# Modulation units of 2 row blocks x 512 columns, two at a time on four column groups; bias rows written later

## Chip, core and metric

The program runs on one core of one Trainium2 chip, in one launch. The metric is the device time of an execution in microseconds (us). The core has a matrix engine (PE, with its weight loads shown apart as PEld), a vector engine (DVE), a scalar engine (ACT), GpSimd (POOL), a queue engine that only issues transfers (SP), and 16 DMA engines that serve all queues.

## Reference

Two layers of a diffusion backbone over 256 latent and 256 context tokens, 1024 wide, in float32. Each layer is feed-forward, token mixing, feed-forward, and each of these is modulated by vectors that come from a conditioning vector. What the change touches is the product that makes these vectors, and the bias table of one of the attentions:

```
c_act = jax.nn.silu(c);  cc_act = jax.nn.silu(c_ctx)
mod  = (c_act  @ lp['w_mod'] + lp['b_mod'])      # w_mod: 1024 x 9216 per layer
modc = (cc_act @ lp['w_mod'] + lp['b_mod'])
ada = lambda t, g, shift, scale: rms_norm(t, g) * (1 + scale) + shift
x = x + 0.5 * m(2) * ffn(ada(x, lp['norm_ffn1'], m(0), m(1)), 'ffn1')
...
bias = rpb[:, dr[:, None, None, :, None], dc[None, :, :, None, :]]
```

## The kernel before

Activations lie transposed: features on the 128 partitions, tokens in columns, 512 columns for both streams. All weights stream from DRAM through four slots `raw[0..3]` of 512 KB, in one fixed order of **units** that `plan_units` lists; unit u uses slot u % 4. SP issues one load for each unit, in order, and waits before it until the slot's last user is through: for a modulation unit until PE has done it (`unit_done`), for a product unit until DVE has made its low part (`lo_made`).

**A product unit** is 1024 rows x 128 columns of a weight. ACT rounds it to `w_hi` (`split_hi`, L631), DVE makes `w_lo` (L641), both two units ahead of PE, and PE does 24 matmuls of 512 columns in the fast float32 format (L690, L691, L696).

**A modulation unit** is 1024 rows x 128 columns of `w_mod`, used by PE as it lands and in full float32: `modulation` (L798) holds a 32 column weight `cact` (the two conditioning vectors, padded with zeros) and streams the 128 columns, once for each of 8 row blocks k. Row block k writes to the 32 output rows of column group k % 4 of PE, so that four partial sums stand in `bank[7]`; the order list has 8 matmuls for such a unit. After four units the bank is full (512 columns). ACT copies it to `mod_row` (L1216), POOL stores the rows to DRAM (L1903), and PE may write the bank again only when it is copied (`mod_copied`, waited for by the first unit of each four). The rows are loaded back later, turned and added up by PE (`turn_modulation`, L810), and DVE makes the vectors of them.

There are 144 modulation units. The first 16 stand alone at the start (the opening), where nothing else can begin before them: two for each eighth of the inputs, which PE turns between them (L974). The other 128 are spread among the gate and up products of the feed-forwards, by the table `MOD_AT`: one modulation unit ahead of each product ("step 2") in seven parts, 104 units in all, and two ahead of each product ("step 3") in one part, 24 units:

```
MOD_AT = {(0, 1, 0): (0, 16, 1), (0, 1, 1): (0, 32, 2), (0, 1, 2): (0, 56, 1),
          (0, 2, 0): (1, 0, 1), (0, 2, 1): (1, 16, 1), (0, 2, 2): (1, 28, 1),
          (1, 1, 0): (1, 44, 1), (1, 1, 1): (1, 60, 1)}
```

The key is (layer, feed-forward, part). A part runs in turns of four products, j = 0 to 3 (gate, up, gate, up), four turns or three. In a turn ACT does in this order: for j = 0 and 2 `split_hi` two products ahead and then SiLU of the gate product (L1203); for j = 1 and 3 `split_hi` and then the rounding of the inner product (L1206). The copy of a full bank stands ahead of the work of j = 3 with step 2, and of j = 1 and j = 3 with step 3, behind the SiLU. The first two products of a feed-forward are done together, block by block as the norm delivers (`first_pair`, L763, L764, L769); with step 2 one modulation unit stands ahead of them and one among them.

POOL also writes the bias rows, a spread copy of `na_rpb`, to DRAM by 8 transfers (L2012); they are read only in the mixing of layer 0.

Of the kernel before, what the change touches and what calls it, by code (L numbers as in the profile page):

```python
# [25 lines left out]
P = 128  # L26
# [142 lines left out]

HALVED = [(0, (1, 2)), (0, "out"), (0, (2, 2)), (1, (1, 2))]  # L170
# [15 lines left out]
def plan_units():  # L186
# [7 lines left out]
    for l in range(LAYERS):  # L194
        if l == 0:
            stage("mod", MOD_FIRST, "mod", DC)
        for ffn in (1, 2):
# [8 lines left out]
            for part, (_, n) in enumerate(PARTS):  # L206
                first["up", l, ffn, part] = len(units)
                for _ in range(2 * n):
                    if (l, ffn, part) in MOD_AT:
                        units.extend(Unit("mod", DC, 1) for _ in range(MOD_AT[l, ffn, part][2]))  # L210
                    units.append(Unit("product", DC, 1))
                stage(("down", l, ffn, part), sweep_steps(l, (ffn, part)), "product", n)
# [10 lines left out]
def build(nc, values, x, c, ctx_tokens, c_ctx, w_mod, b_mod, norm_ffn1, ffn1_w_gate, ffn1_w_up, ffn1_w_down,  # L223
# [7 lines left out]
    with ExitStack() as ctx:  # L231
# [303 lines left out]
        def _(sp):  # L535
# [6 lines left out]
            def load(u, i, per, *sources):  # L542
# [11 lines left out]
                for rows, src in sources:  # L554
                    sp.dma_start(raw[unit.slot][:, rows[0]:rows[1], :], src).then_inc(loaded[unit.slot], 16)
# [16 lines left out]
            for l in range(LAYERS):  # L572
                if l == 0:
                    stage(first["mod"], MOD_FIRST, lambda j: [((0, DC), columns(w_mod, 0, j * P))])
                for ffn in (1, 2):
# [16 lines left out]
                    for part, (c0, n) in enumerate(PARTS):  # L592
# [6 lines left out]
                        def turn_loads(i, per):  # L599
                            for j in range(4):  # L600
                                for q in range(ahead):
                                    load(u0 + step * j + q, i, per, ((0, DC), columns(
                                        w_mod, extra[0], i * (4 * ahead * P) + (extra[1] + ahead * j + q) * P)))
                                load(u0 + step * j + step - 1, i, per,
                                     ((0, DC), columns((wg, wu)[j % 2], l, i * (2 * P) + (c0 + j // 2) * P)))
# [48 lines left out]
        def at(u0, j, i, step=1):  # L654

            j = step * j + step - 1
# [20 lines left out]
        def _(pe):  # L677
# [110 lines left out]
            def modulation(u, i, per, j, m):  # L788
# [25 lines left out]
            def up(l, ffn, part, n):  # L814
# [9 lines left out]
                def body(i):  # L824
                    start = 0
                    if part == 0 and isinstance(i, int) and i == 0:
                        m0 = mod_first.get((l, ffn, part))
                        if step == 2:
                            modulation(u0, 0, (0, 0), 0, m0)
                        for j in range(2):  # L830

                            pe.wait_ge(silu_done if j == 0 else inner_made, c0)
                        first_pair(at(u0, 0, 0, step), at(u0, 1, 0, step), n, (l, ffn),
                                   (lambda: modulation(u0 + 2, 0, (0, 0), 1, m0)) if step == 2 else None)
# [1230 lines left out]
```

## Time and profile before

| | |
|---|---|
| median of 3 runs | 2385.78 us (2379.91 to 2389.27) |
| profiled execution | 2382.76 us, span 2380.8 us |
| PE busy | 2257.0 us, 95% |
| PE weight loads / DVE / ACT / POOL busy | 78% / 50% / 38% / 10% |
| PE clock granted, mean | 0.98 |
| DMA | 340.83 MB, mean 143 GB/s |

Busy time is that of the profiled execution, and its span leaves out some 2 us around it. PE is nearly always busy, so that time can be won only in PE's own work or in its few stretches of waiting.

### The profile page before, as it was taken

The numbers are of one execution on the slowest core, as the hardware profiler recorded it, in microseconds if no ns is written. First come the engines' busy times: TensorE is split into PE (matmuls) and PEld (weight loads), VectorE is DVE, ScalarE is ACT, GpSimd is POOL, SyncE is SP. The second block draws the span as 40 slices with busy tenths as digits, with TensorE's granted clock in tenths as the row PEclk, the third lists the DMA queues.
The fourth block names the chain that finished last, engine by engine and source line by source line (L and its number), as shares of the span: only waits on it lengthen the run. The fifth ranks groups of instructions, "written<-read, shape, count | busy, mean of one in ns | idle before, by whom it ended". The sixth has DMA issues, their size and how long they took to land. (4 is left out here: it accounts for less than half of the span.)

```text
span 2380.8 us, 36412 instructions
## 1 busy us (share of the span) xinstructions
PE 2257.0 (95%) x14113; PEld 1851.9 (78%) x14113; DVE 1179.6 (50%) x1848; ACT 902.6 (38%) x1415; POOL 238.2 (10%) x347
## 2 busy tenths in 40 slices
PE   4999899999999989999999999999999899988998
PEld 3777677888766667877777797777889777788998
DVE  1432232496377546743333364333337848775554
ACT  2321222353455442532222253222235446634444
POOL 2000000150000001200000020000005101110000
PEclk8999999999999999999999999999999999989999
DMA  9554746553333335555454655545335445564663
GB/s 275 149 165 125 190 126 175 165 133 102 93 100 97 93 107 150 153 152 164 116 152 137 171 165 157 158 119 155 111 97 153 119 109 144 146 182 142 179 181 119
DMA packets 618095, 340.83 MB, mean 143 GB/s; under 512 B 15307, under 2 KB 609719, under 8 KB 617815
## 3 DMA queue, kind: packets, MB, share of 16 engines
q1 hardware_dynamic: 603648, 305.18, 45.9%
q0 software_dynamic: 12848, 29.37, 4.5%
q10 hardware_dynamic: 1446, 4.18, 0.5%
q8 instruction: 104, 1.70, 0.3%
q14 instruction: 49, 0.39, 0.0%
HBM read 326.50 MB, written 12.94 MB: 143 GB/s over the span
## 5 line engine op out<-in xcount | busy, mean ns | idle before, releaser
L641 DVE TENSOR_TENSOR w_lo<-raw,w_hi 128x1024 fp32r<-128x1024 f32 (+1 forms) x444 | 544.5, 1227 | 925.2 <-ACT w_hi L631 539.6
L631 ACT ACTIVATE w_hi<-raw 128x1024 fp32r<-128x1024 f32 (+1 forms) x444 | 462.4, 1041 | 951.8 <-PE bank L691 366.1
L690 PE MATMUL bank<-h_hi,w_hi 128*128 128x512 f32 (+1 forms) x1856 | 661.4, 368 | 12.0 <-DVE h_lo L1510 10.7
L691 PE MATMUL bank<-h_lo,w_hi 128*128 128x512 f32 (+1 forms) x1856 | 643.2, 359 | 0.0
L690 PEld LDWEIGHTS bank<-h_hi,w_hi 128*128 128x128 f32 x1856 | 354.2, 191 | 86.4 <-issue 34.6
L696 PE MATMUL bank<-h_hi,w_lo 128*128 128x512 f32 (+1 forms) x1856 | 395.5, 356 | 5.1 <-DVE w_lo L641 5.1
L691 PEld LDWEIGHTS bank<-h_lo,w_hi 128*128 128x128 f32 x1856 | 355.6, 192 | 48.2 <-issue 0.5
L696 PEld LDWEIGHTS bank<-h_hi,w_lo 128*128 128x128 f32 x1856 | 314.2, 190 | 54.5 <-DVE w_lo L641 5.9
L690 PE MATMUL bank<-inner_hi,w_hi 128*128 128x256 f32 (+1 forms) x896 | 270.7, 327 | 11.3 <-DVE inner_lo L1575 10.9
L691 PE MATMUL bank<-inner_lo,w_hi 128*128 128x256 f32 (+1 forms) x896 | 268.8, 324 | 0.0
L690 PEld LDWEIGHTS bank<-inner_hi,w_hi 128*128 128x128 f32 x896 | 169.0, 189 | 30.9 <-DVE inner_lo L1575 15.1
L705 PE MATMUL bank<-h_hi,w_hi 128*128 128x512 f32 (+1 forms) x512 | 169.9, 351 | 12.1 <-ACT wa L1369 7.7
L691 PEld LDWEIGHTS bank<-inner_lo,w_hi 128*128 128x128 f32 x896 | 169.2, 189 | 15.4
L706 PE MATMUL bank<-h_lo,w_hi 128*128 128x512 f32 (+1 forms) x512 | 165.0, 341 | 0.0
L696 PE MATMUL bank<-inner_hi,w_lo 128*128 128x256 f32 (+1 forms) x896 | 163.8, 324 | 0.0
L696 PEld LDWEIGHTS bank<-inner_hi,w_lo 128*128 128x128 f32 x896 | 134.3, 189 | 15.3
L1903 POOL DMA_DIRECT2D mod_rows<-mod_row x72 | 40.6, 565 | 965.9 <-ACT mod_row L1216 964.2
L705 PEld LDWEIGHTS bank<-h_hi,w_hi 128*128 128x128 f32 x512 | 98.3, 192 | 46.7 <-ACT gstage L1369 19.1
L798 PE MATMUL bank<-raw,cact 128*32 128x128 f32 x2304 | 96.7, 293 | 31.0 <-DMA raw<-in_w_mod_dram 19.5
L1206 ACT ACTIVATE inner_hi<-wb 128x512 fp32r<-128x512 f32 (+3 forms) x88 | 50.9, 579 | 177.9 <-DVE wb L1571 177.9
L798 PEld LDWEIGHTS bank<-raw,cact 128*32 128x32 f32 x2304 | 59.2, 115 | 75.2 <-issue 60.1
L1591 DVE SCALAR_TENSOR_TENSOR X<-bank,gatev,X 128x256 f32<-128x256 f32 x192 | 87.9, 479 | 46.3 <-PE bank L696 46.0
(226 smaller groups left out, 2407.3 us busy)
## 6 DMA issues: line engine op xcount, KB each, us to landing
raw<-in_w_mod_dram SPq DMA_DIRECT2D x144, 512.0 KB, 4.0
raw<-in_w_in_dram SPq DMA_DIRECT2D x108, 512.0 KB, 4.0
raw<-in_ffn_w_gate_dram SPq DMA_DIRECT2D x88, 512.0 KB, 4.9
raw<-in_ffn_w_up_dram SPq DMA_DIRECT2D x88, 512.0 KB, 4.9
raw<-in_ffn_w_down_dram SPq DMA_DIRECT2D x88, 512.0 KB, 4.1
raw<-in_ffn_w_down_dram SPq DMA_DIRECT2D x32, 384.0 KB, 3.5
raw<-in_w_out_dram SPq DMA_DIRECT2D x24, 512.0 KB, 4.1
raw<-in_w_branch_dram SPq DMA_DIRECT2D x16, 512.0 KB, 5.2
```

Of the source, the lines that this page charges most:

```text
L631: act.activation(w_hi[n % 2][:, 0:unit.rows, :], raw[unit.slot][:, 0:unit.rows, :], ACT.Copy).then_inc(hi_made, 1)
L641: dve.tensor_tensor(w_lo[n % 2][:, 0:unit.rows, :], raw[unit.slot][:, 0:unit.rows, :], w_hi[n % 2][:, 0:unit.rows, :].bitcast(F32), ALU.su ...
L690: pe.matmul(psum, w_hi[s][:, row0 + k, :], hi, start=(k == 0), stop=False)
L691: mm = pe.matmul(psum, w_hi[s][:, row0 + k, :], lo, start=False, stop=False)
L696: mm = pe.matmul(psum, w_lo[s][:, row0 + k, :], rhs(k)[0], start=False, stop=(k == rows - 1))
L705: pe.matmul(psum, w_hi[s][:, k, :], h_hi[:, k, 0:n], start=(k == 0), stop=False)
L706: mm = pe.matmul(psum, w_hi[s][:, k, :], h_lo[:, k, 0:n], start=False, stop=False)
L798: mm = pe.matmul(bank[7][rows, j * P:(j + 1) * P], cact[:, k, :], raw[unit.slot][:, k, :], start=(k < 4), stop=(k >= 4))
L1206: act.activation(inner_hi[:, bass.ds(i * 2 + j // 2, 1), 0:n], wb[:, (j // 2) % 2:(j // 2) % 2 + 1, 0:n], ACT.Copy).then_inc(inner_hi_made, 1)
L1591: ins = dve.scalar_tensor_tensor(out=X[:, d % DC, stream_cols(st)], in0=bank[4 + d % 2][:, stream_cols(st)], scalar=gatev[:, gate_i, d % D ...
L1903: pool.dma_start(mod_rows[l, s, :, bass.ds(chunk0 * P, 4 * P)], mod_row[s::32, :]).then_inc(mod_stored, 16)
```

## The change

A modulation unit now has 2 row blocks x 512 columns, where it had 8 row blocks x 128. Four units still make a full bank: unit 4a + j of them holds row blocks 2j and 2j + 1 of the same 512 columns. It has 2 matmuls of 512 columns, to two of the four column groups: units 0 and 2 of a four to groups 0 and 1, units 1 and 3 to groups 2 and 3. In DRAM the pieces of a load are 2 KB long, where they were 512 bytes. With step 2 the order of a turn becomes two modulation units and then two products (`TURN_ORDER`); with step 3 it stays as it was. The two modulation units of the first two products now both stand ahead of them. The 8 transfers of the bias rows move in POOL's program from behind the load of the first vectors to behind the load of portion (0, "gate"), in the feed-forward.

```diff
+TURN_ORDER = {1: ["p0", "p1", "p2", "p3"],
+              2: ["m0", "m1", "p0", "p1", "m2", "m3", "p2", "p3"],
+              3: ["m0", "m1", "p0", "m2", "m3", "p1", "m4", "m5", "p2", "m6", "m7", "p3"]}
...
+def in_turn(step, kind, j):
+
+    return TURN_ORDER[step].index(kind + str(j))
...
+                    dst = raw[unit.slot][:, rows[0]:rows[1], :]
+                    if unit.kind == "mod":
+                        dst = raw[unit.slot][:, :, :].rearrange("p r c -> p (r c)").rearrange("p (k n) -> p k n", k=2)
+                    sp.dma_start(dst, src).then_inc(loaded[unit.slot], 16)
+
+            def mod_rows_of(l, col, a):
+
+                return w_mod[l].rearrange("(k p) n -> p k n", p=P)[:, 2 * a:2 * a + 2, bass.ds(col, 4 * P)]
...
-                for k in range(DC):
+                two = raw[unit.slot][:, :, :].rearrange("p r c -> p (r c)").rearrange("p (k n) -> p k n", k=2)
+                for k in (2 * j, 2 * j + 1):
                     rows = slice(32 * (k % 4), 32 * (k % 4) + 32)
-                    mm = pe.matmul(bank[7][rows, j * P:(j + 1) * P], cact[:, k, :], raw[unit.slot][:, k, :],
-                                   start=(k < 4), stop=(k >= 4))
+                    mm = pe.matmul(bank[7][rows, :], cact[:, k, :], two[:, k % 2, :], start=(k < 4), stop=(k >= 4))
...
-                        m0 = mod_first.get((l, ffn, part))
-                        if step == 2:
-                            modulation(u0, 0, (0, 0), 0, m0)
+                        for q in range(2 * (step - 1)):
+                            modulation(u0 + in_turn(step, "m", q), 0, (0, 0), q % 4, mod_first[l, ffn, part] + q // 4)
...
-            for l in range(LAYERS):
-                for h in range(4):
-
-                    row = na_rpb[l, h, NA_ROWS - ROWS, 0:1]
-                    src = bass.AP(row.tensor, row.offset, [[2 * NA_COLS - 1, 2 * ROWS - 1], [0, GRID_W], [1, P]])
-                    rows_written.done(pool.dma_start(bias_rows[l, h], src), "all")
             for key in sorted(MOD_AT):
                 l, chunk0, ahead = MOD_AT[key]
                 if key == (0, 1, 1):
                     load_modulation(0, "gate")
+                    write_bias_rows()
```

On PE, in the first turn with step 2 (part (0, 1, 0)), the order before, from the end of the first two products (L763 to L769) on, is a modulation unit, a product (L690, L691, L696), a modulation unit, a product:

```order
L798 MATMUL bank<-raw,cact 32x128 x8
L690 MATMUL bank<-h_hi,w_hi 128x512
L691 MATMUL bank<-h_lo,w_hi 128x512
...
L696 MATMUL bank<-h_hi,w_lo 128x512 x8
L798 MATMUL bank<-raw,cact 32x128 x8
L690 MATMUL bank<-h_hi,w_hi 128x512
L691 MATMUL bank<-h_lo,w_hi 128x512
...
L696 MATMUL bank<-h_hi,w_lo 128x512 x8
```

and at the same place of the changed kernel, whose lines L817, L708, L709 and L714 are L798, L690, L691 and L696 of before:

```order
L817 MATMUL bank<-raw,cact 32x512 x4
L708 MATMUL bank<-h_hi,w_hi 128x512
L709 MATMUL bank<-h_lo,w_hi 128x512
...
L714 MATMUL bank<-h_hi,w_lo 128x512 x8
L708 MATMUL bank<-h_hi,w_hi 128x512
L709 MATMUL bank<-h_lo,w_hi 128x512
...
L714 MATMUL bank<-h_hi,w_lo 128x512 x8
```

Two units of 8 short matmuls have become 4 long ones in a row, and the two products stand next to each other.

On SP, the loads of that part's first turn before:

```order
L555 DMA raw<-in_w_mod_dram 128x8x128
L555 DMA raw<-in_ffn_w_gate_dram 128x8x128
L555 DMA raw<-in_w_mod_dram 128x8x128
L555 DMA raw<-in_ffn_w_up_dram 128x8x128
```

and in the changed kernel, where the first row also holds the 16 units of the opening:

```order
L567 DMA raw<-in_w_mod_dram 128x2x512 x18
L567 DMA raw<-in_ffn_w_gate_dram 128x8x128
L567 DMA raw<-in_ffn_w_up_dram 128x8x128
L567 DMA raw<-in_w_mod_dram 128x2x512 x2
```

The gate load now stands behind two modulation loads, where one was ahead of it.

On POOL, the transfers around the load of the first vectors before:

```order
L1914 DMA scores<-mod_rows 16x8x128
L2012 DMA bias_rows<-in_na_rpb_dram 448x1x128 x8
L2028 UNCONDITIONAL_BRANCH
```

and in the changed kernel, around the second such load, one loop of stores later:

```order
L1933 DMA scores<-mod_rows 8x8x128
L1954 DMA bias_rows<-in_na_rpb_dram 448x1x128 x8
L2051 UNCONDITIONAL_BRANCH
```

The 8 transfers now follow the modulation stores of part (0, 1, 0) and stand ahead of those of part (0, 1, 1).

## Rows read from the trace of the kernel before

**Rows 1.** The page: span, busy time and share of each engine
```profile
span 2380.8 us, 36412 instructions
PE 2257.0 (95%) x14113; PEld 1851.9 (78%) x14113; DVE 1179.6 (50%) x1848; ACT 902.6 (38%) x1415; POOL 238.2 (10%) x347
```

**Rows 2.** PE by time, step 2: start, us, line, tiles, count
```profile
131.71 0.51 PE L690 MATMUL bank<-h_hi,w_hi 128*128 128x512 f32 x1
...
137.42 0.64 PE L798 MATMUL bank<-raw,cact 128*32 128x128 f32 x16
137.99 0.51 PE L690 MATMUL bank<-h_hi,w_hi 128*128 128x512 f32 x1
```

**Rows 3.** PE by time, a part without modulation: first matmuls of products
```profile
1699.90 0.39 PE L690 MATMUL bank<-h_hi,w_hi 128*128 128x512 f32 x1
...
1705.34 0.39 PE L690 MATMUL bank<-h_hi,w_hi 128*128 128x512 f32 x1
```

**Rows 4.** PE by time, step 3: a pair of units between products
```profile
232.44 0.50 PE L690 MATMUL bank<-h_hi,w_hi 128*128 128x512 f32 x1
...
238.11 1.08 PE L798 MATMUL bank<-raw,cact 128*32 128x128 f32 x32
239.12 0.50 PE L690 MATMUL bank<-h_hi,w_hi 128*128 128x512 f32 x1
```

**Rows 5.** PE by time, attention: float32 on two column groups
```profile
704.44 0.38 PE L1045 MATMUL bank<-probs_t,v_tok 128*64 128x256 f32 x1
704.44 0.38 PE L1045 MATMUL bank<-scores,v_tok 128*64 128x256 f32 x1
...
705.73 0.38 PE L1045 MATMUL bank<-probs_t,v_tok 128*64 128x256 f32 x1
```

**Rows 6.** All engines by time, the opening
```profile
19.31 1.08 PE L798 MATMUL bank<-raw,cact 128*32 128x128 f32 x16 [0.74 <-DMA raw<-in_w_mod_dram]
20.32 1.97 PE L974 MATMUL bank<-cst,x_in 128*128 128x128 f32 x8
...
41.20 0.64 PE L798 MATMUL bank<-raw,cact 128*32 128x128 f32 x16 [1.05 <-DMA raw<-in_w_mod_dram]
...
48.79 0.56 POOL L1914 DMA_DIRECT2D scores<-mod_rows  x1 [4.49 <-DMA mod_rows<-mod_row]
49.34 6.38 POOL L2012 DMA_DIRECT2D bias_rows<-in_na_rpb_dram  x8
...
61.12 0.55 PE L763 MATMUL bank<-h_hi,w_hi 128*128 128x256 f32 x1 [2.85 <-DVE h_lo L1539]
```

**Rows 7.** DMA queues by packets, MB, share; 2 to 42 us
```profile
q1 hardware_dynamic: 18010, 9.08, 90.7%
```

**Rows 8.** The same, 46 to 50 us (a load of long rows)
```profile
DMA packets 631, 1.64 MB, mean 411 GB/s; under 512 B 72, under 2 KB 522, under 8 KB 530
...
q10 hardware_dynamic: 101, 1.40, 84.4%
```

**Rows 9.** ACT and SP by time, step 2
```profile
119.42 0.37 SPq L555 DMA_DIRECT2D raw<-in_w_mod_dram  x1
...
125.23 1.06 ACT L631 ACTIVATE w_hi<-raw 128x1024 fp32r<-128x1024 f32 x1 [2.55 <-DMA raw<-in_ffn_w_gate_dram]
```

**Rows 10.** ACT, SP and PE by time, step 3: a late copy
```profile
256.04 0.37 SPq L555 DMA_DIRECT2D raw<-in_w_mod_dram  x1
256.66 1.36 SPq L555 DMA_DIRECT2D raw<-in_ffn_w_gate_dram  x1
...
262.68 1.06 ACT L631 ACTIVATE w_hi<-raw 128x1024 fp32r<-128x1024 f32 x1 [5.57 <-DMA raw<-in_ffn_w_gate_dram]
...
264.85 1.94 PE L798 MATMUL bank<-raw,cact 128*32 128x128 f32 x32 [2.90 <-ACT mod_row L1216]
```

**Rows 11.** PE's waits: for whom, us, times, longest
```profile
PE bank L798 <- DMA raw<-in_w_mod_dram: 19.5, 10, 10.9
PE bank L798 <- ACT mod_row L1216: 10.6, 5, 2.9
```

More of the change, by code:

```diff
@@ L207, in plan_units @@
                 first["up", l, ffn, part] = len(units)
[L208 to L211, printed above, removed]
+                step = 1 + MOD_AT[l, ffn, part][2] if (l, ffn, part) in MOD_AT else 1
+                for _ in range(n // 2):
+                    units.extend(Unit("mod" if name[0] == "m" else "product", DC, 1) for name in TURN_ORDER[step])
                 stage(("down", l, ffn, part), sweep_steps(l, (ffn, part)), "product", n)
@@ L573, in _ @@
                 if l == 0:
-                    stage(first["mod"], MOD_FIRST, lambda j: [((0, DC), columns(w_mod, 0, j * P))])
+                    for j in range(MOD_FIRST):
+                        load(first["mod"] + j, 0, (0, 0), ((0, DC), mod_rows_of(0, j // 4 * 4 * P, j % 4)))
                 for ffn in (1, 2):
@@ L599, in turn_loads @@
                         def turn_loads(i, per):
[L600 to L605, printed above, removed]
+                            for at_unit, name in enumerate(TURN_ORDER[step]):
+                                j = int(name[1])
+                                if name[0] == "m":
+                                    source = mod_rows_of(extra[0], i * (4 * ahead * P) + (extra[1] + j // 4 * 4) * P, j % 4)
+                                else:
+                                    source = columns((wg, wu)[j % 2], l, i * (2 * P) + (c0 + j // 2) * P)
+                                load(u0 + at_unit, i, per, ((0, DC), source))
                         turn_loads(0, (0, 0))
@@ L654, in at @@
         def at(u0, j, i, step=1):
[L656 removed]
+            j = in_turn(step, "p", j)
             return (u0 + 4 * step * i + j, 0, (0, 0)) if isinstance(i, int) else (u0 + j, i, (4 * step, 4))
@@ L826, in body @@
                     if part == 0 and isinstance(i, int) and i == 0:
[L827 to L829 removed]
+                        for q in range(2 * (step - 1)):
+                            modulation(u0 + in_turn(step, "m", q), 0, (0, 0), q % 4, mod_first[l, ffn, part] + q // 4)
                         for j in range(2):
                             pe.wait_ge(silu_done if j == 0 else inner_made, c0)
[L833 to L834 removed]
+                        first_pair(at(u0, 0, 0, step), at(u0, 1, 0, step), n, (l, ffn))
                         start = 2
[L836 to L840 removed]
+                    for at_unit, name in enumerate(TURN_ORDER[step]):
+                        j = int(name[1])
+                        if start and at_unit <= in_turn(step, "p", 1):
+                            continue
+                        if name[0] == "m":
+                            u, ii, per = (u0 + 4 * step * i + at_unit, 0, (0, 0)) if isinstance(i, int) else (u0 + at_unit, i, (4 * step, 4))
+                            modulation(u, ii, per, j % 4, i * (step - 1) + (mod_first[l, ffn, part] + j // 4))
+                            continue
                         if not (isinstance(i, int) and i == 0):
@@ L963, in _ @@
                         for j in range(4):
-                            modulation(*at(first["mod"], j, i), j, i or None)
+                            modulation(first["mod"] + 4 * i + j, 0, (0, 0), j, i or None)
                         if i == 1:
@@ L1926, in small_loads, with write_bias_rows @@
                 layer_loads.done(pool.dma_start(wdt_raw[:, :, :], w_in[l].rearrange("(c p) n -> p c n", p=P)[:, :, DT_COL:GATE_COL]), l)
+            def write_bias_rows():
+                for l in range(LAYERS):
+                    for h in range(4):
+                        row = na_rpb[l, h, NA_ROWS - ROWS, 0:1]
+                        src = bass.AP(row.tensor, row.offset, [[2 * NA_COLS - 1, 2 * ROWS - 1], [0, GRID_W], [1, P]])
+                        rows_written.done(pool.dma_start(bias_rows[l, h], src), "all")
             def neighbourhood_bias(l):
```

12 lines of the change are left out of this document (3 added, 9 removed).

## The prediction, made before the changed kernel ran

> **What bounds the kernel now.** I read the page first: PE is busy for 2257.0 of 2380.8 us [rows 1], so time comes out of PE's own work or out of its few waits. Next PE's waits, longest first, of which two touch this change: 19.5 us for modulation loads, in the opening, and 10.6 us in five waits for the copy of the full bank, which all lie in the part with step 3 [rows 11]. Then PE by time, in three kinds of places. With step 2 a product starts every 6.28 us (131.71 to 137.99), with one modulation unit in between, and PE never waits [rows 2]. In a part without modulation a product starts every 5.44 us (1699.90 to 1705.34) [rows 3]. So a modulation unit that stands alone costs PE 6.28 - 5.44 = 0.84 us. With step 3 two units stand together, and where nothing waits the next product starts after 6.68 us (232.44 to 239.12) [rows 4]: the pair costs 1.24 us, not 1.68. The second unit costs 0.40 us; the other 0.44 us of a lone unit is the price of going from full-width products to 32 column weights and back.
>
> **What a unit's time is made of.** The order lists 8 matmuls for a unit and the trace 16 rows [rows 2], so a float32 matmul goes through PE twice. In the attention, passes of 256 columns on two column groups start in pairs, one for each group, and six pairs on from 704.44 stands 705.73, so the next pair starts 0.215 us later [rows 5]: 0.84 ns a column and pass, and the groups work at the same time, although in the program both passes of the one stand ahead of the other's. A modulation unit is 16 passes x 128 columns x 0.84 ns = 1.72 us on one group, and the second unit of a pair costs 0.40 us, about a fourth: all four groups run at once.
>
> **The change, part by part.**
>
> *Matmul shape.* A pair of new units is 4 matmuls x 2 passes x 512 columns = 4096 column passes, and a pair of old ones 2 x 16 x 128 = 4096. With one matmul on each of the four groups that is 4096 x 0.84 / 4 = 0.86 us, plus the 0.4 us of going over: about 1.25 us, which is the 1.24 us of the old pair. I take 1.24. Shape alone gives nothing; weight loads fall to a fourth, but they were hidden (PEld is at 78%, under PE). The bounds: 1.1 if part of the 0.4 was weight loads, 2.1 if the second unit waits for the first (0.86 + 0.86 + 0.4).
>
> *Order with step 2.* This is the main term. 104 units in seven parts become 52 pairs: 52 x (2 x 0.84 - 1.24) = 22.9 us less. In three of them (the first turn of a feed-forward) both units come ahead of the first two products, where PE waits anyway for the norm, as in the opening (2.85 us idle before 61.12) [rows 6]; I add 1 us for that (bounds 0 and 2).
>
> *Order with step 3.* The 12 pairs stay, and cost the same. The five waits: the copy is behind a `split_hi` of ACT that waits for the gate load. That was issued at 256.66, behind a modulation load at 256.04; ACT had it at 262.68, and after SiLU and copy PE went on at 264.85 after 2.90 us idle [rows 10]. Now the first unit of a pair ends with the second, 0.4 us later than before, and its slot's next load is issued that much later; against it the modulation load ahead of the gate load is shorter (next term) by 0.5 us. I take 0, with bounds of 5 us more and 8 us less: five waits, each 0.5 us longer, or 1 us shorter with the slower clock that follows them gone. After such a wait the pair takes 1.94 us instead of 1.08 [rows 4, 10].
>
> *DMA pieces.* In the opening PE waits for the loads: 12 units from 19.31 to 41.20, so 1.82 us each [rows 6]. From 2 to 42 us the loads' queue has 18010 packets of 504 bytes on average and 90.7% of 16 engines: 0.907 x 16 x 40 / 18010 = 32.2 ns each [rows 7]. The long rows of 13.9 KB take 0.844 x 16 x 4 / 101 = 535 ns [rows 8]. On the line between the two, 2 KB take 90 ns, against 129 ns for four pieces of 512 bytes: 0.70, so 1.28 us a unit. All 16 units would save 16 x 0.54 = 8.6 us. Not all of it arrives: a lone new unit holds PE for 0.86 us at full clock (before 0.64), twice that at half clock, and its slot comes free that much later; and between fours PE turns inputs for up to 1.97 us [rows 6], while only four loads can be under way. I take 5 us less, bounds 0 and 9.
>
> The Trainium skill ("DMA: Bandwidth & Descriptors", Specifications) gives 512 bytes as the size from which a transfer reaches line rate. By that the longer pieces would give 0 in the opening and the sum would be 5 us higher. The trace speaks against it: 411 GB/s in the stretch of long rows [rows 8], against 504 bytes in 32.2 ns, and it is the trace that I follow.
>
> *Bias rows.* They were issued from 49.34 on for 6.38 us, behind the load of the first vectors at 48.79 [rows 6], which alone is on the way to the first product. Moved, they lie in a down phase, where there are no modulation units and so no stores for POOL to issue behind them; a delay of 6 us there is covered by the rest of that phase, 8 products of over 5 us. I take 0, bounds 1 us either way.
>
> **Does a new wait appear with step 2?** This is what I am least sure of. Both slots of a pair come free together, so SP issues two modulation loads, then gate, then up. Before, gate was second: from the issue of the modulation load (119.42) to ACT's `split_hi` (125.23) it took 5.8 us [rows 9]. Now: 5.8 + 1.28 for the second modulation load - 0.5 for the shorter first = 6.6 us. From there to PE's next modulation unit it takes `split_hi`, SiLU and copy, 262.68 to 264.85 = 2.2 us [rows 10]. With 0.3 us from the end of the pair to the issue that is 9.1 us, and PE needs the bank after two products, 10.9 us. So 1.8 us are to spare, once in each of 26 turns. If the up load takes its share of the engines at the same time (1.8 us), nothing is left.
>
> **Sum.** 2382.8 (the profiled execution) - 22.9 - 1 - 5 + 0 + 0 = 2353.9 us. The median of the three runs lies 3 us above that execution, so I say 2355.
>
> **Rivals.**
>
> *The copy comes late with step 2.* The gate load is third or worse in a burst of four, and PE waits for the bank in every turn. Each microsecond costs 26 us; with 0.8 us it is 21 us, and the result 2375. For it: the same chain does stall PE with step 3 [rows 10]. Against it: there PE has one product to cover it, here two. Chance 0.12.
>
> *The column groups don't fill (slower).* If a pass on one group holds back whatever stands behind it in the program, the new order is bad: both passes of a row block stand ahead of the next group's first. Then a pair takes five steps of 512 x 0.84 = 0.43 us, 2.15 + 0.4 = 2.5 us. It decides from 1.68 us a pair on, above which step 2 loses. With 2.5: 52 x 0.82 + 12 x 1.26 = 58 more, - 6, so 2435; with the milder form, the second unit behind the first, 2.1 us: 22 + 10 - 6, so 2409. Against it: the old units kept the same order of passes and filled the groups, as the 0.40 us and the attention's rows show [rows 4, 5]. Chance 0.10.
>
> The Trainium skill has such a rule ("TensorE: Matmul & The Clock Gate", The mechanism): matmuls keep program order strictly in start and end. By that the old unit would have taken 9 steps of 0.107 us, 0.96 us, and the attention's rows would not alternate; the trace does not agree.
>
> *The longer pieces don't help,* the opening stays: 2360. It could be that the long rows are a poor guide to 2 KB. Chance 0.15.
>
> *More than forecast.* Shorter modulation loads take the step 3 waits under the length after which PE's clock is slower, and the opening gains all: 2353.9 - 4 - 8 = 2342. The two shortest of the five waits need only a little. Chance 0.13.
>
> **How the numbers follow.** The forecast has 0.50, between 2345 and 2366. With the four rivals that makes 1. The range 2338 to 2378 holds all but the slower rival and some of the tails. A measurement of this kernel tells about 0.5%, 12 us, from no change. Faster by more than that (under 2371): forecast, no help from the pieces, more than forecast, and a third of the late copy: 0.82. Within 0.5%: the rest of the late copy and a little of the mild form: 0.09. Slower: 0.09.
>
> **What the profile of the changed kernel would show.** Step 2: from the first matmul of a gate product to that of the next gate product 12.1 us (before 12.56), with 8 rows of modulation in one stretch of some 1.0 us, and no wait for the copy. Step 3: periods and five waits much as before. Opening: the last modulation unit done near 37 us (before 41.84), and 61.12 becomes about 56. Wrong it would be if the pair's stretch is nearer 2 us, or if PE's waits show the copy of the bank 26 times more.

## The result

The changed kernel takes 2357.18 us (median of 4 executions, 2353.26 to 2359.01), the kernel before, run beside it, 2385.03 us (4 executions, 2379.91 to 2389.27). The ratio is 0.9882, with a 95% interval of 0.9859 to 0.9905: 1.2% less time, where the forecast was 2355. The profiled execution took 2353.26 us, its span is 2351.3 us.

The page of the changed kernel, first its line of the span, then busy time of each engine [rows 1]:

```profile
span 2351.3 us, 32904 instructions
...
PE 2236.1 (95%) x12385; PEld 1807.3 (77%) x12385; DVE 1178.7 (50%) x1848; ACT 899.8 (38%) x1415; POOL 239.1 (10%) x347
```

PE is busy for 20.9 us less, and its span is 29.5 us shorter: most of the gain is work that PE no longer does, the rest is time in which it waited. The other engines do what they did.

PE by time with step 2 [rows 2]; the first two rows are pairs of modulation units, then the first matmuls of the gate and the up product, then the next pair:

```profile
124.60 1.06 PE L817 MATMUL bank<-raw,cact 128*32 128x512 f32 x8
...
136.70 1.06 PE L817 MATMUL bank<-raw,cact 128*32 128x512 f32 x8
137.70 0.50 PE L708 MATMUL bank<-h_hi,w_hi 128*128 128x512 f32 x1
...
143.28 0.39 PE L708 MATMUL bank<-h_hi,w_hi 128*128 128x512 f32 x1
...
148.81 1.07 PE L817 MATMUL bank<-raw,cact 128*32 128x512 f32 x8
```

Two products and their modulation take 148.81 - 136.70 = 12.11 us, where two periods of 6.28 were 12.56. All 8 passes of a pair are in one stretch of 1.06 us. Without modulation two products take 2 x 5.44 = 10.88 us [rows 3], so the pair costs 12.11 - 10.88 = 1.23 us.

The opening [rows 6]. The first row is the kernel before, its first two units of the 16. The rest is the changed kernel: the first unit and the next three, the last four, the transposes behind them, the first pair of units of the feed-forward, the first product:

```profile
14.32 2.29 PE L798 MATMUL bank<-raw,cact 128*32 128x128 f32 x32 [10.86 <-DMA raw<-in_w_mod_dram]
...
11.81 1.92 PE L817 MATMUL bank<-raw,cact 128*32 128x512 f32 x4 [8.38 <-DMA raw<-in_w_mod_dram]
14.26 5.42 PE L817 MATMUL bank<-raw,cact 128*32 128x512 f32 x12 [0.52 <-DMA raw<-in_w_mod_dram]
...
33.54 1.05 PE L817 MATMUL bank<-raw,cact 128*32 128x512 f32 x4 [0.56 <-DMA raw<-in_w_mod_dram]
34.84 1.05 PE L817 MATMUL bank<-raw,cact 128*32 128x512 f32 x4 [0.24 <-DMA raw<-in_w_mod_dram]
36.28 1.05 PE L817 MATMUL bank<-raw,cact 128*32 128x512 f32 x4 [0.39 <-DMA raw<-in_w_mod_dram]
37.59 1.05 PE L817 MATMUL bank<-raw,cact 128*32 128x512 f32 x4 [0.25 <-DMA raw<-in_w_mod_dram]
38.57 1.09 PE L993 MATMUL bank<-cst,x_in 128*128 128x128 f32 x8
...
54.05 1.94 PE L817 MATMUL bank<-raw,cact 128*32 128x512 f32 x8 [0.75 <-DVE gain L1640]
57.98 0.55 PE L781 MATMUL bank<-h_hi,w_hi 128*128 128x256 f32 x1 [1.99 <-DVE h_lo L1558]
```

The last four units come (37.59 - 33.54) / 3 = 1.35 us apart. The 1.82 us of before were read over twelve units, from the fourth to the last; over the same twelve the changed kernel takes (37.59 - 17.75) / 12 = 1.65 us (the fourth starts at 17.75, within the row of 12 passes, which is three units). The first unit starts at 11.81, where it was 14.32, the last at 37.59, where it was 41.20, and the first product at 57.98, where it was 61.12. The second unit of the first pair lies in a wait: PE still idles 1.99 us behind the pair.

The loads' queue from 2 to 42 us, packets, MB and share of the 16 engines [rows 7]:

```profile
q1 hardware_dynamic: 6103, 10.05, 77.0%
```

A packet now holds 1647 bytes on average and takes 0.770 x 16 x 40 / 6103 = 80.7 ns, where one of 504 bytes took 32.2. The queue's share fell from 90.7% to 77.0%: between the quicker loads it now stands empty at times.

PE's waits that touch the change: for whom, us, times, longest [rows 11]:

```profile
PE bank L817 <- DMA raw<-in_w_mod_dram: 12.8, 10, 8.4
...
PE bank L817 <- ACT mod_row L1235: 10.4, 6, 2.8
```

The wait for modulation loads is 6.7 us shorter. The wait for the copy of the bank is the same 10.4 us, and 10.2 of it are again five waits in the part with step 3. The sixth, of 0.3 us, is the only one with step 2.

Where the time came from, by the first modulation row of each part (before in [rows 6] for the opening; the starts of the parts stand in the same view of both kernels):

| stretch | before, us | after, us | difference |
|---|---|---|---|
| start to first product | 61.12 | 57.98 | -3.1 |
| (0, 1, 0), step 2, 16 units | 216.05 - 57.19 = 158.86 | 208.17 - 54.05 = 154.12 | -4.7 |
| (0, 1, 1), step 3, 24 units | 348.56 - 216.05 = 132.51 | 338.42 - 208.17 = 130.25 | -2.3 |
| (0, 1, 2), step 2, 16 units, and the mixing | 1014.51 - 348.56 = 665.95 | 1002.02 - 338.42 = 663.60 | -2.4 |
| (0, 2, 0), step 2, 16 units | 1166.66 - 1014.51 = 152.15 | 1148.70 - 1002.02 = 146.68 | -5.5 |
| (0, 2, 1), step 2, 12 units | 1276.61 - 1166.66 = 109.95 | 1255.96 - 1148.70 = 107.26 | -2.7 |
| (0, 2, 2), step 2, 16 units | 1428.36 - 1276.61 = 151.75 | 1402.94 - 1255.96 = 146.98 | -4.8 |
| (1, 1, 0), step 2, 16 units | 1579.12 - 1428.36 = 150.76 | 1550.44 - 1402.94 = 147.50 | -3.3 |
| (1, 1, 1), step 2, 12 units, and all the rest | 2380.8 - 1579.12 = 801.68 | 2351.3 - 1550.44 = 800.86 | -0.8 |

By 0.45 us a pair, a part of 16 units should give 3.6 us and one of 12 units 2.7. The rows scatter around that by up to 2 us each, and much of the scatter is not the change. In (0, 2, 2) the granted clock was 0.51 from 1401.2 to 1404.7 us before, and 1.00 throughout after. In the last row the part itself gives its 2.7 us, but in the work behind it the changed kernel loses 1.8. Of these, 1.6 are in one place, where the same work has this clock (before, then after; the columns are the stretch, its us, busy us and count of PE, PEld, DVE, ACT and POOL, the granted clock, the DMA share and GB/s):

```profile
1870.84:1879.46 8.62, 6.64 (x33) 5.43 (x31) 6.20 (x8) 5.27 (x8) 0.00 (x0) 1.00 0.68 184
1839.45:1849.67 10.22, 8.24 (x32) 6.57 (x31) 6.21 (x8) 5.27 (x8) 0.00 (x0) 0.83 0.56 154
```

### The profile page after: what moved, and what is told of

It is laid out like the page before. It is cut to its first block and busy times, and to the rows that moved or that the text cites. A ratio compares the mean times of both kernels' runs of the same rounds, so it can differ in the third digit from the quotient of the medians.

```text
span 2351.3 us, 32904 instructions
## 1 busy us (share of the span) xinstructions
PE 2236.1 (95%) x12385; PEld 1807.3 (77%) x12385; DVE 1178.7 (50%) x1848; ACT 899.8 (38%) x1415; POOL 239.1 (10%) x347
## 5 line engine op out<-in xcount | busy, mean ns | idle before, releaser
L708 PE MATMUL bank<-h_hi,w_hi 128*128 128x512 f32 (+1 forms) x1856 | 654.4, 365 | 13.1 <-DVE h_lo L1529 11.3
L709 PE MATMUL bank<-h_lo,w_hi 128*128 128x512 f32 (+1 forms) x1856 | 642.2, 358 | 0.0
L708 PEld LDWEIGHTS bank<-h_hi,w_hi 128*128 128x128 f32 x1856 | 355.3, 191 | 115.9 <-issue 56.5
L714 PE MATMUL bank<-h_hi,w_lo 128*128 128x512 f32 (+1 forms) x1856 | 395.5, 356 | 4.4 <-DVE w_lo L659 4.4
L709 PEld LDWEIGHTS bank<-h_lo,w_hi 128*128 128x128 f32 x1856 | 355.7, 192 | 48.4 <-issue 0.5
L714 PEld LDWEIGHTS bank<-h_hi,w_lo 128*128 128x128 f32 x1856 | 314.2, 190 | 53.8 <-DVE w_lo L659 5.2
L708 PE MATMUL bank<-inner_hi,w_hi 128*128 128x256 f32 (+1 forms) x896 | 270.0, 326 | 11.3 <-DVE inner_lo L1594 10.9
L709 PE MATMUL bank<-inner_lo,w_hi 128*128 128x256 f32 (+1 forms) x896 | 267.5, 323 | 0.0
L708 PEld LDWEIGHTS bank<-inner_hi,w_hi 128*128 128x128 f32 x896 | 168.3, 188 | 31.1 <-DVE inner_lo L1594 15.1
L709 PEld LDWEIGHTS bank<-inner_lo,w_hi 128*128 128x128 f32 x896 | 168.2, 188 | 15.4
L714 PE MATMUL bank<-inner_hi,w_lo 128*128 128x256 f32 (+1 forms) x896 | 163.3, 323 | 0.0
L714 PEld LDWEIGHTS bank<-inner_hi,w_lo 128*128 128x128 f32 x896 | 133.7, 188 | 15.4
L817 PE MATMUL bank<-raw,cact 128*32 128x512 f32 x576 | 87.6, 623 | 24.0 <-DMA raw<-in_w_mod_dram 12.8
L733 PE MATMUL bank<-h_hi,w_lo 128*128 128x512 f32 (+1 forms) x512 | 106.6, 351 | 0.0
```

Source lines behind the costliest of these rows:

```text
L708: pe.matmul(psum, w_hi[s][:, row0 + k, :], hi, start=(k == 0), stop=False)
L709: mm = pe.matmul(psum, w_hi[s][:, row0 + k, :], lo, start=False, stop=False)
L714: mm = pe.matmul(psum, w_lo[s][:, row0 + k, :], rhs(k)[0], start=False, stop=(k == rows - 1))
L733: mm = pe.matmul(psum, w_lo[s][:, k, :], h_hi[:, k, 0:n], start=False, stop=(k == DC - 1))
L817: mm = pe.matmul(bank[7][rows, :], cact[:, k, :], two[:, k % 2, :], start=(k < 4), stop=(k >= 4))
```

## The experiments

Five runs do one part of the change, undo one or bend one, and three put the modulation copy elsewhere. Each still computes the whole reference. Ratios are to the kernel before, run beside it. It had medians of 2385.03 us beside the changed kernel, 2383.36 beside e1 to e4, 2387.16 beside e5 and e6 and 2386.95 beside e7 and e8, so a difference of medians between two of these groups is known to some 4 us only.

### Order alone: e1_order_only

The kernel before with the new order of units with step 2. The units keep 8 row blocks x 128 columns, the bias rows stay in the opening. Its edit is the change's `TURN_ORDER` and the loops that follow it, with these lines kept from before:

```diff
+              2: ["m0", "m1", "p0", "p1", "m2", "m3", "p2", "p3"],
...
                 for k in range(DC):
                     rows = slice(32 * (k % 4), 32 * (k % 4) + 32)
                     mm = pe.matmul(bank[7][rows, j * P:(j + 1) * P], cact[:, k, :], raw[unit.slot][:, k, :],
```

> The kernel before with nothing but the new order of turns with step 2 (two modulation units, then two products; both units ahead of the first two products of a feed-forward); units of 8 row blocks x 128 columns, pieces of 512 bytes, bias rows in the opening. Theory (the gain is the order): a pair of old units costs 1.24 us where two lone ones cost 1.68, so 52 pairs give 23 us, a product pair with its modulation every 12.1 us, no gain in the opening; 2359 to 2363 us. Rival (the wide units make the gain): little, 2380 or more. Rival (the copy comes late when the loads come in bursts): waits of PE for the copy in most of 26 turns, 2370 and more.

Measured: 2361.83 us (2352.48 to 2367.11), ratio 0.9893 (0.9861 to 0.9925). PE by time, the first product of the kernel and two pairs with step 2:

```profile
63.96 0.55 PE L778 MATMUL bank<-h_hi,w_hi 128*128 128x256 f32 x1 [1.99 <-DVE h_lo L1555]
...
118.52 1.08 PE L813 MATMUL bank<-raw,cact 128*32 128x128 f32 x32
130.63 1.08 PE L813 MATMUL bank<-raw,cact 128*32 128x128 f32 x32
```

Pair to pair is 12.11 us, as with the new shape. In its profile PE never waits for the copy with step 2, so the copy does not come late. The order alone gives most of the gain, 21.5 of the 27.9 us between medians, and the opening stays where it was or later. Its executions scatter by 15 us, more than any other kernel's here, so it does not tell the 5 us of the opening from none.

### Shape alone: e2_shape_only

The changed kernel with the old order with step 2.

```diff
-              2: ["m0", "m1", "p0", "p1", "m2", "m3", "p2", "p3"],
+              2: ["m0", "p0", "m1", "p1", "m2", "p2", "m3", "p3"],
```

> The changed kernel with the old order of turns with step 2 (one modulation unit ahead of each product). A lone unit of 2 matmuls uses two column groups only. Theory (time on the groups plus 0.4 us for going over): 0.86 + 0.4 = 1.26 us where the old lone unit costs 0.84, so a product every 6.70 us, 104 x 0.42 = 44 us more than before, less 3 in the opening and 2 with step 3: 2422 us. Rival (the 0.4 us is made of the narrow weight loads, which are a fourth now): 0.86 + 0.1, a product every 6.4 us, 2392. Rival (shape does not matter): 2380.

Measured: 2418.28 us (2416.39 to 2421.51), ratio 1.0141 (1.0121 to 1.0161). PE by time with step 2, a lone unit and the product behind it, twice:

```profile
122.32 1.05 PE L817 MATMUL bank<-raw,cact 128*32 128x512 f32 x4
123.30 0.50 PE L708 MATMUL bank<-h_hi,w_hi 128*128 128x512 f32 x1
...
128.97 1.05 PE L817 MATMUL bank<-raw,cact 128*32 128x512 f32 x4
129.95 0.50 PE L708 MATMUL bank<-h_hi,w_hi 128*128 128x512 f32 x1
```

A product starts every 129.95 - 123.30 = 6.65 us, so a lone unit costs 6.65 - 5.44 = 1.21 us, almost what a pair costs. A lone unit of the new shape has work for two of the four column groups only, and leaves the other two idle. The new shape by itself is a loss of 35 us against the median of the kernel before beside it. It is worth having only with the new order.

### Bias rows in the opening again: e3_bias_back

```diff
             load_modulation(0, "in")
+            write_bias_rows()
...
                 if key == (0, 1, 1):
                     load_modulation(0, "gate")
-                    write_bias_rows()
```

> The changed kernel with the 8 transfers of the bias rows back in the opening, behind the load of the first vectors. Theory: they are hidden in either place, 0 to 1 us more than the changed kernel, the first product of the first feed-forward starts within 0.5 us of it. Rival: they held up the transfers of the opening, and their move gave 2 to 4 us of the 3 us by which the opening is shorter; then this kernel's first product starts near 61 us.

Measured: 2361.40 us (2356.24 to 2362.25), ratio 0.9897 (0.9877 to 0.9917). Its interval and that of the changed kernel overlap, and its first product starts at 57.62 us, against 57.98: the place of the bias rows does nothing in the opening. The rest of its 4 us is within the spread of executions, though 0 to 1 had been expected; in the profiled one the waits for the copy with step 3 are longer (11.9 us in five). It also has two such waits with step 2, of 0.5 and 0.8 us. PE by time at the first:

```profile
124.25 1.07 PE L817 MATMUL bank<-raw,cact 128*32 128x512 f32 x8
136.87 1.07 PE L817 MATMUL bank<-raw,cact 128*32 128x512 f32 x8 [0.45 <-ACT mod_row L1235]
```

The bias rows are long written at that time, so this wait is no effect of theirs: what is to spare between copy and next pair differs from turn to turn. In the changed kernel POOL issues the bias rows in the down phase, behind the load of vectors:

```profile
161.73 0.60 POOL L1933 DMA_DIRECT2D scores<-mod_rows  x1 [3.24 <-DMA mod_rows<-mod_row]
162.32 6.38 POOL L1954 DMA_DIRECT2D bias_rows<-in_na_rpb_dram  x8
```

### The new shape in short pieces: e4_pieces_512

The changed kernel, but a modulation unit is loaded by two transfers of 256 KB in pieces of 512 bytes.

```diff
-                        dst = raw[unit.slot][:, :, :].rearrange("p r c -> p (r c)").rearrange("p (k n) -> p k n", k=2)
-                    sp.dma_start(dst, src).then_inc(loaded[unit.slot], 16)
+                        for k in range(2):
+                            sp.dma_start(raw[unit.slot][:, :, :].rearrange("p (c k) n -> p k c n", k=2)[:, k],
+                                         src[:, k].rearrange("p (c n) -> p c n", n=P)).then_inc(loaded[unit.slot], 16)
```

> The changed kernel with the modulation units of the same shape on PE, but stored in the slot so that their pieces are 512 bytes again, in two transfers of 256 KB for each unit. Theory (the opening's 3 us come from the longer pieces): the opening is as long as before or, since a unit now holds PE and its slot longer, up to 2 us longer; step 2 stays at 12.1 us a pair; 3 to 5 us more than the changed kernel, 2360 to 2363 us. Rival (the pieces' length does nothing): the same as the changed kernel.

Measured: 2362.74 us (2360.73 to 2364.74), ratio 0.9908 (0.9890 to 0.9926). The loads' queue from 2 to 42 us:

```profile
q1 hardware_dynamic: 18390, 9.13, 92.3%
```

and PE by time, the last units of the opening and the first product:

```profile
39.04 1.05 PE L819 MATMUL bank<-raw,cact 128*32 128x512 f32 x4 [0.77 <-DMA raw<-in_w_mod_dram]
40.82 1.05 PE L819 MATMUL bank<-raw,cact 128*32 128x512 f32 x4 [0.72 <-DMA raw<-in_w_mod_dram]
...
61.78 0.55 PE L783 MATMUL bank<-h_hi,w_hi 128*128 128x256 f32 x1 [1.99 <-DVE h_lo L1560]
```

The opening is back at that of before: the last twelve units come every 1.83 us (18.89 to 40.82), the first product is at 61.78, with packets of 496 bytes that take 0.923 x 16 x 40 / 18390 = 32.1 ns. So it is the length of the pieces, and not the shape of the matmuls, that shortens the opening, by 61.78 - 57.98 = 3.8 us. The edit also makes two transfers of each load; the kernel before has one, and the same rate, so their number does not matter here. The two spans are 9.9 us apart, and the other 6.1 us are spread: 2.0 in the part with step 3, where PE waits 7.2 us for `w_hi` (six times), 2.1 in (0, 1, 0), and the rest in the later parts; with step 2 pair to pair stays 12.11 us (116.89 to 129.00).

### Both row blocks of a unit on one column group: e6_one_group

Unit j of a four puts both row blocks on column group j, so that a pair uses two groups.

```diff
-                    rows = slice(32 * (k % 4), 32 * (k % 4) + 32)
-                    mm = pe.matmul(bank[7][rows, :], cact[:, k, :], two[:, k % 2, :], start=(k < 4), stop=(k >= 4))
+                    rows = slice(32 * j, 32 * j + 32)
+                    mm = pe.matmul(bank[7][rows, :], cact[:, k, :], two[:, k % 2, :], start=(k % 2 == 0), stop=(k % 2 == 1))
```

> The changed kernel with both row blocks of a modulation unit on one column group (unit j on group j), so that a pair of units has two groups at work instead of four. Theory (groups work side by side, each takes its own passes in turn): a pair takes 4 passes x 0.43 = 1.72 us plus 0.4, 2.1 us instead of 1.24; step 2 has a pair of products every 13.0 us; 64 pairs x 0.86 = 55 us more, 2410 us. Rival (strict program order: the second group's first pass waits for the first group's last): 3 us plus 0.4 a pair, 14.3 us, 2490 us. Rival (groups don't matter, the sum of columns does): no change.

Measured: 2408.82 us (2406.80 to 2410.84), ratio 1.0091 (1.0072 to 1.0109). PE by time with step 2:

```profile
130.16 1.92 PE L817 MATMUL bank<-raw,cact 128*32 128x512 f32 x8
132.01 0.50 PE L708 MATMUL bank<-h_hi,w_hi 128*128 128x512 f32 x1
...
143.16 1.92 PE L817 MATMUL bank<-raw,cact 128*32 128x512 f32 x8
145.00 0.50 PE L708 MATMUL bank<-h_hi,w_hi 128*128 128x512 f32 x1
```

Pair to pair is 145.00 - 132.01 = 12.99 us, so the pair costs 2.11 us. Each of the two groups has four passes, 4 x 512 x 0.84 = 1.72 us, and 0.39 remain. In program order all four passes of the first unit stand ahead of the second unit's. If the second unit's first pass could not start ahead of the first unit's last, the pair would have taken seven steps of 0.43 us and 0.4, 3.4 us, and pair to pair 14.3. They did not hold it back. PE between 130.17 and 130.60 us:

```profile
130.16 0.63 PE L817 MATMUL bank<-raw,cact 128*32 128x512 f32 x2
```

Two passes of 0.62 us each lie within 0.63 us, one for each unit, while three more of the first unit are still to come. The groups work side by side although the program has one unit's passes ahead of the other's.

The Trainium skill ("TensorE: Matmul & The Clock Gate", The mechanism) has matmuls start and end strictly in program order. This run's 12.99 us, where strict order asks for 14.3, does not agree.

### The copy ahead of the split with step 3: e5_copy_first

The 10.4 us that PE waits for the copy are the same before and after. The copy stands behind a `split_hi` that waits for a gate load, though the bank is full long before. Here it is put one step of the turn earlier, with step 3 alone.

```diff
-                        if step > 1 and (step - 1) * (j + 1) % 4 == 0:
+                        early = j + 1 if step == 3 else j
+                        if step > 1 and (step - 1) * (early + 1) % 4 == 0:
...
-                            copy_modulation(u0 + in_turn(step, "m", (step - 1) * (j + 1) - 1) + 1 + i * (4 * step),
-                                            i * (step - 1) + (mod_first[l, ffn, part] + (step - 1) * (j + 1) // 4 - 1))
+                            copy_modulation(u0 + in_turn(step, "m", (step - 1) * (early + 1) - 1) + 1 + i * (4 * step),
+                                            i * (step - 1) + (mod_first[l, ffn, part] + (step - 1) * (early + 1) // 4 - 1))
```

> The changed kernel, and with step 3 ACT copies the full bank ahead of the rounding of the gate weights two products ahead and of SiLU, instead of behind them. Theory (the five or six waits for the copy come from its place in ACT's order, behind a gate load that lands late): PE's 10.4 us of waits for the copy fall to 1 us or less, and with them the slower clock after the longer ones, 9 to 14 us less than the changed kernel, 2343 to 2348 us. Rival (PE then waits for the next thing, the gate weights or the up weights themselves): half of that or less, with new waits of PE for the rounded weights in the same part.

Measured: 2342.06 us (2339.30 to 2344.76), ratio 0.9813 (0.9800 to 0.9827). This beats both kernels, by 15 us the changed one, a little over the 9 to 14 expected. First the changed kernel: four stretches with step 3 from one pair of units to the next, each behind a wait of PE for the copy of 2.19, 1.37, 2.81 and 2.32 us. The columns are those of the two rows on the clock in the section on the result:

```profile
239.33:245.99 6.66, 6.66 (x32) 4.58 (x33) 0.14 (x1) 0.00 (x0) 1.13 (x2) 1.00 0.58 163
255.08:261.74 6.66, 6.66 (x32) 4.58 (x32) 0.14 (x1) 0.00 (x0) 1.13 (x2) 1.00 0.68 198
271.56:279.82 8.26, 8.26 (x32) 5.75 (x32) 0.26 (x2) 1.06 (x1) 1.13 (x2) 0.79 0.66 192
288.88:297.12 8.24, 8.24 (x32) 5.77 (x32) 0.37 (x2) 1.06 (x1) 1.13 (x2) 0.79 0.65 177
```

Behind the two longer waits the same 32 rows take 8.25 us instead of 6.66, at a granted clock of 0.79: each of these waits costs 1.6 us once more after it has ended. The length of the wait alone does not decide it. In the kernel before, waits of 2.08 and 2.06 us were followed by a clock of 0.77 and 0.79; in e4_pieces_512 one of 2.86 us was followed by 1.00. The whole part, of the changed kernel in the same view:

```profile
208.20:338.40 130.20, 117.49 (x529) 84.38 (x528) 36.45 (x48) 30.04 (x39) 6.83 (x12) 0.97 0.58 171
```

and of e5_copy_first:

```profile
209.30:328.10 118.80, 114.24 (x529) 81.93 (x528) 36.45 (x48) 29.94 (x39) 6.83 (x12) 1.00 0.63 187
```

The part is 11.4 us shorter with as many instructions, and that is the whole difference of the two spans, 2351.3 - 2339.9. PE's busy time has 3.25 us less of it, at a clock of 1.00 instead of 0.97. The rest is idle time. ACT by time shows how the copy (L1236) now ends ahead of the split that waits:

```profile
247.24 0.63 ACT L1226 ACTIVATE inner_hi<-wb 128x512 fp32r<-128x512 f32 x1 [1.89 <-DVE wb L1591]
247.78 0.58 ACT L1236 ACTIVATE mod_row<-bank 128x512 f32<-128x512 f32 x1
250.55 1.06 ACT L649 ACTIVATE w_hi<-raw 128x1024 fp32r<-128x1024 f32 x1 [2.19 <-DMA raw<-in_ffn_w_gate_dram]
```

and PE's waits in this part of e5_copy_first are

```profile
PE bank L708 <- ACT w_hi L649: 3.6, 6, 1.1
PE bank L708 <- DVE inner_lo L1595: 0.8, 1, 0.8
```

The 10.2 us for the copy are gone, and 1.9 us of them come back as more short waits for `w_hi` (3.6, against 1.7 in the changed kernel): -10.2 - 3.25 + 1.9 = -11.5 us. What is late next is the load itself. The medians are 15 us apart and the profiled executions 11.4; the changed kernel's profile is that of its fastest execution.

### The copy first with both steps: e7_copy_first_both

As above with `early = j + 1` for step 2 too.

> The modulation copy of every turn, of step 2 and of step 3, goes onto ScalarE ahead of the turn's last gate split and SiLU (the run that moved it in step 3 alone gave 2342.06 us). My theory: in step 2 no matmul waits for the copy in the changed kernel (1.07 us are left between the copy's end and the next pair), so moving it there gives nothing: 2338 to 2346 us, within 0.3% of 2342.06, a gap of 12.1 us from pair to pair in step 2. Rival A, that step 2 too loses to the copy somewhere that the profile did not name: some 0.2 us in each of 52 turns, 10 us less, near 2332. Rival B, that the copy now delays the last gate split of step 2 (0.6 us on ScalarE ahead of it) and the products that wait for it: 52 x 0.6 = 31 us at most, near 2373, with a new wait of PE for w_hi in step 2.

Measured: 2340.71 us (2338.01 to 2343.89), ratio 0.9814 (0.9793 to 0.9835), which is e5_copy_first's. Pair to pair stays 12.11 us (123.04 to 135.15). With step 2 there was next to nothing to win: in e5_copy_first's profile PE waits for the copy there twice, 0.9 us in all, and here never.

### The copy later with step 2: e8_copy_late_step2

The changed kernel, with step 2's copy behind the last `split_hi` of the turn, not ahead of it.

```diff
-                        if step > 1 and (step - 1) * (j + 1) % 4 == 0:
+                        if step == 3 and (step - 1) * (j + 1) % 4 == 0:
...
                         split_hi(act, n0 + j + 2 + (4 * i if straight else 0), ii, per)
+                        if step == 2 and (step - 1) * (j + 1) % 4 == 0:
+
+                            copy_modulation(u0 + in_turn(step, "m", (step - 1) * (j + 1) - 1) + 1 + i * (4 * step),
...
```

> The changed kernel with step 2's modulation copy moved behind one more operation of ScalarE, the last gate split, which puts it 1.06 us later. In the changed kernel the copy ends 1.07 us before the next pair of modulation units wants its slot. My theory: the 1.06 us use up the spare and nothing more: a wait of 0 to 0.3 us in each of 52 turns, 2357 to 2373 us, within 0.7% of the changed kernel, and this is the point from which a later copy costs. Rival, that the spare is larger than it looks because the pair's own issue is what holds it: no wait at all, 2353 to 2360 us. Rival, that the late copy holds whole turns: over 1 us in each, 2410 us or more.

Measured: 2358.79 us (2352.96 to 2363.07), ratio 0.9887 (0.9859 to 0.9915), the changed kernel's. ACT by time in the changed kernel, one turn with step 2 [rows 9]; SP had issued the pair's loads from 125.85 on, and PE's next pair starts at 136.70:

```profile
133.59 1.06 ACT L649 ACTIVATE w_hi<-raw 128x1024 fp32r<-128x1024 f32 x1 [6.30 <-DMA raw<-in_ffn_w_gate_dram]
134.56 0.58 ACT L1222 ACTIVATE wa<-bank 128x512 f32<-128x512 f32 x1
135.04 0.59 ACT L1235 ACTIVATE mod_row<-bank 128x512 f32<-128x512 f32 x1
135.51 1.06 ACT L649 ACTIVATE w_hi<-raw 128x1024 fp32r<-128x1024 f32 x1
```

and in e8_copy_late_step2, where PE's next pair starts at 137.73:

```profile
136.02 1.06 ACT L649 ACTIVATE w_hi<-raw 128x1024 fp32r<-128x1024 f32 x1
136.99 0.58 ACT L1239 ACTIVATE mod_row<-bank 128x512 f32<-128x512 f32 x1
```

The copy ends 136.70 - 135.63 = 1.07 us ahead of the pair in the one, and 137.73 - 137.57 = 0.16 us ahead in the other. Over all 26 turns with step 2 (the copy comes once a turn; the 52 of the expectation is the number of pairs), PE now has nine waits for it, of 0.2 to 1.4 us and 5.6 us in all, where the changed kernel has one of 0.3 us. So the spare is about 1 us in a common turn, all of it is used here, and a copy later than that is where the rival of the late copy starts to cost. The 5.6 us do not show in the medians, which are 1.6 us apart.

## Why the prediction was right, step by step

**The sum.** The mechanism held in its main term. That the total came within 2.2 us is in part luck. By the two profiles the kernel gained 29.5 us, where 28.9 were forecast: about 23.4 from the order, 3.1 in the opening instead of 5, 2.3 in the part with step 3 where 0 was taken, 2.7 in the parts that start a feed-forward instead of 1, and a loss of some 2 us in the clock and the rest, which the forecast did not have.

**The main term (22.9 us).** It held. A pair in a row costs 1.23 us where 1.24 was taken, and 52 x (2 x 0.84 - 1.23) = 23.4 us. The order alone brought 12.11 us from pair to pair, so the term belongs to the order and not to the shape.

**Matmul shape (0).** It held. The pair costs 1.23 us in the old shape (e1_order_only) and in the new. The 0.40 us of going over is not made of weight loads: the old pair has 32 passes and the new one 8, and what remains over the 0.86 us of columns is 0.37 in both.

**First pairs (1 us, bounds 0 and 2).** No gain of this kind is shown. Over eight pairs a part of 16 units should give 3.6 us; the three parts that start a feed-forward give 4.7, 5.5 and 3.3, together 2.7 more than three times that, but (0, 2, 2), which starts none, gives 1.2 more too. e2_shape_only has both units in their old places and is the better measure. Its three parts are 9.7, 10.0 and 9.1 us longer than the changed kernel's, 28.8 in all, where eight pairs of 2 x 1.21 - 1.23 us each ask for 28.6. So nothing clear is left for the place of the first pair. Most of the 1.9 us that (0, 2, 0) gave over its 3.6 is one wait of 1.5 us for `wa` in the profile of before, which e2_shape_only does not have either. The 1 us was not borne out.

**DMA pieces (5 us, bounds 0 and 9).** The step was right and its size hopeful. The 1.28 us a unit is nearly what loads in an unbroken row reach, 1.35 for the last four. Over the twelve units that the 1.82 was read from it is 1.65, as the queue is not always full; against that the first unit starts 2.5 us sooner. The last unit ends at 38.64 us, not near 37, and the two profiles differ by 3.1 us in the opening. The prediction also set 0.86 us, the columns alone, against a row of 0.64; the row of a lone new unit is 1.05 us at full clock. The first product starts at different times from one execution to the next: 61.12, 63.96 and 61.78 in the three profiles with short pieces, and 57.98, 56.38, 57.62, 57.58, 56.42 and 58.49 in six with long ones (e6_one_group, which holds PE longer for each unit, has 60.05). The means are 62.3 and 57.4, so 4.9 us less. These kernels differ in more than the pieces, but most of it comes behind the first product. The one pair that differs in the pieces alone gives 3.8 (e4_pieces_512).

The Trainium skill ("DMA: Bandwidth & Descriptors", Specifications) has transfers at line rate from 512 bytes on. e4_pieces_512 against the changed kernel says otherwise here. With pieces of 512 bytes, 496 a packet on average, 496 bytes in 32.1 ns are 15.5 bytes a ns, 1647 bytes in 80.7 ns are 20.4.

**Step 3 (0, bounds -8 and +5).** It held for the changed kernel: 10.6 us of waits before, 10.2 after, 132.5 us and 130.3 us for the part. That is one execution of each. In the profiles of e1, e2, e3, e4 and e8, which leave its copy where it was, this part lasts from 130.1 to 137.0 us, at mean granted clocks between 0.93 and 1.00, the largest spread that I found within the program. So the 2.3 us are no sure gain. What I had not seen was the chance: all of these waits are one instruction in the wrong place on ACT.

**Bias rows (0).** It held, within what e3_bias_back can tell.

**The new wait with step 2.** It did not appear (one wait of 0.3 us in the profile), but the spare was overrated. I had 0.3 + 6.6 + 2.2 us against 10.9; the row has 0.2 + 7.7 + 2.0 against 11.0, so 1.07 us were left, not 1.8. The term that was small is the gate load's, 7.7 us from the first issue to the split instead of 6.6. That the up load, issued 0.5 us behind the gate load and under way with it, takes its share of the engines fits this; I had named it and not counted it, and no run shows it by itself. e3_bias_back shows two turns in which nothing was left.

**The rivals.** The copy late with step 2: no (e8_copy_late_step2 shows how near it was). The groups don't fill: no, and e6_one_group shows that program order does not hold back another group. The longer pieces don't help: no. More than forecast: no, the waits with step 3 did not get shorter; taken away whole, with e5_copy_first, they are worth 15 us by the medians and 11.4 by the profiles.

## What to carry to other kernels

Work in 32 column groups beside full-width matmuls has a price for each change between them, here 0.37 us: put such pieces next to each other, and give each stretch work for all four groups, before asking about their shape. When an engine that is off the critical path does a small thing that the critical one waits for, look at what stands ahead of it in its program: here a copy of 0.6 us behind an operation that waited for a load cost 10 us of waits and 3 us of slower clock, and moving it by one place took all but 2 us of it away.

## What the hardware showed that I had not expected

Going from full-width matmuls to 32 columns and back costs the same in all forms tried: 0.84 - 0.43 = 0.41 us for a lone old unit, 1.23 - 0.86 = 0.37 for an old pair (32 passes of 128 columns) and for a new pair (8 passes of 512), 1.21 - 0.86 = 0.35 for a lone new unit, 2.11 - 1.72 = 0.39 for a pair on two groups. Over these forms it does not depend on the number or the width of the matmuls. Whether a longer row of units, four at a time, would pay it only once was not tried, and which step of the change-over takes the time stays open.

Waits of PE of 2.81 and 2.32 us in the changed kernel were followed by a mean granted clock of 0.79 until the next pair of units, those of 2.19 and 1.37 us by 1.00. So PE ran at the lower of its two levels (1.2 and 2.4 GHz) for a part of the stretches behind the longer ones, and the price was 1.6 us each. The same 1.6 us turn up far from the change, at some 1843 us in layer 1, in the changed kernel and not in the profile of before. Single profiles differ by such stretches.
